# Moving buffers in SBUF: parameters in front, split weights 32 bytes apart modulo 512

## What is computed

```python
# layer 1
h = rms_norm(x, pre_mix_norm)
proj = h @ w_in                       # 1024 x 6688, split into q,k,v,z,... of two recurrences
mix = concat([gated_delta_rule(...), ssd(...)]) @ w_out
x = x + rms_norm(mix, post_mix_norm)
u = causal_dwconv(rms_norm(x, pre_ffn_norm) @ w_up, ffn_conv_w, ffn_conv_b)   # 1024 x 5632
gate, up = split(u, 2)
x = x + rms_norm((silu(gate) * up) @ w_down, post_ffn_norm)                   # 2816 x 1024
# layers 2 and 3: stick-breaking attention with pooling, then gated linear attention,
# each followed by the same kind of feed-forward block
```

## Time and profile before

| | |
|---|---|
| timed runs | 2160.79, 2166.26, 2170.13 us (median 2166.26) |
| profiled execution: span from first to last instruction | 2157.8 us |
| its own time outside the span | not recorded; the median of the timed runs is 8.5 us above the span |
| matmul engine busy | 2109.7 us, 9,776 matmuls |
| weight loads busy | 1698.0 us, beside the matmuls |
| DVE, ACT, POOL busy | 1213.1, 906.3, 325.6 us |
| DMA | 188.96 MB, 27.6% of 16 engines' time |

### The profile page before, as it was taken

How to read it: one execution, slowest core, us unless ns; L and a number is a source line. 1 busy time by engine, 2 the same in 40 slices (tenths; PEclk the granted TensorE clock), 3 DMA queues, 4 the chain that set the end, 5 groups by cost and what they waited for, 6 DMA issues and landing times.

```text
span 2157.8 us, 26841 instructions
## 1 busy us (share of the span) xinstructions
PE 2109.7 (98%) x9776; PEld 1698.0 (79%) x9776; DVE 1213.1 (56%) x1663; ACT 906.3 (42%) x1282; POOL 325.6 (15%) x266
## 2 busy tenths in 40 slices
PE   6999999999999999999999999999999999999999
PEld 5778888878868888877766888888878878888887
DVE  5898755765366665226544566653354465666522
ACT  6883445434254444224564444442242354444311
POOL 0002121220122222001302122210000011222100
PEclk9999999999999999999999999999999999999999
DMA  7323322122323233221111333232222122323321
GB/s 234 93 77 92 86 74 69 59 69 69 101 65 97 94 94 120 94 86 59 59 40 50 97 94 94 95 116 96 80 77 88 51 78 88 98 97 97 114 94 66
DMA packets 81481, 188.96 MB, mean 88 GB/s; under 512 B 19824, under 2 KB 40432, under 8 KB 81392
## 3 DMA queue, kind: packets, MB, share of 16 engines
q1 hardware_dynamic: 81392, 187.75, 27.6%
HBM read 178.28 MB, written 9.44 MB: 87 GB/s over the span
## 4 chain that ended last, share of the span: by engine, by line
PE 92%; DVE 4%; ACT 2%; issue 1%; DMA 0%; POOL 0%; SPq 0%; ACTq 0%; DVEq 0%; POOLq 0%
PE acc L253 23%; PE acc L255 23%; PE acc L254 23%; PE bank L1726 1%; PE bank L1245 1%; PE bank L229 1%; PE bank L230 1%; PE bank L231 1%; PE acc L2634 1%; PE acc L2633 1%; PE acc L2632 1%; PE bank L2017 1%; PE bank L253 1%; PE bank L255 1%; PE bank L254 1%
## 5 line engine op out<-in xcount | busy, mean ns | idle before, releaser
L253 PE MATMUL acc<-HH,whi 128*128 128x512 f32 x1600 | 642.1, 401 | 7.1 <-DVE wlo L191 4.5
L255 PE MATMUL acc<-HH,wlo 128*128 128x512 f32 x1600 | 624.4, 390 | 0.0
L254 PE MATMUL acc<-HL,whi 128*128 128x512 f32 x1600 | 623.5, 390 | 0.0
L185 ACT ACTIVATE whi<-raw 128x1024 fp32r<-128x1024 f32 (+1 forms) x293 | 324.2, 1108 | 573.5 <-PE acc L255 543.4
L191 DVE TENSOR_TENSOR wlo<-raw,whi 128x1024 fp32r<-128x1024 f32 (+1 forms) x293 | 400.9, 1369 | 287.8 <-ACT whi L185 287.8
L253 PEld LDWEIGHTS acc<-HH,whi 128*128 128x128 f32 x1600 | 301.1, 188 | 74.1 <-DVE wlo L191 11.0
L255 PEld LDWEIGHTS acc<-HH,wlo 128*128 128x128 f32 x1600 | 300.5, 188 | 64.0
L254 PEld LDWEIGHTS acc<-HL,whi 128*128 128x128 f32 x1600 | 301.1, 188 | 62.0 <-issue 4.1
L253 PE MATMUL acc<-FH,whi 128*128 128x512 f32 x528 | 208.9, 396 | 0.0
L255 PE MATMUL acc<-FH,wlo 128*128 128x512 f32 x528 | 208.6, 395 | 0.0
L254 PE MATMUL acc<-FL,whi 128*128 128x512 f32 x528 | 208.5, 395 | 0.0
(11 more groups left out here) (394 smaller groups left out, 2673.1 us busy)
## 6 DMA issues: line engine op xcount, KB each, us to landing
raw<-w SPq DMA_DIRECT2D x257, 512.0 KB, 3.5
raw<-w SPq DMA_DIRECT2D x48, 704.0 KB, 4.0
X<-x SPq DMA_DIRECT2D x4, 512.0 KB, 5.2
x_dram<-small SPq DMA_DIRECT2D x8, 256.0 KB, 4.4
xt_dram<-small SPq DMA_DIRECT2D x8, 256.0 KB, 3.6
a_dram<-l_am SPq DMA_DIRECT2D x8, 256.0 KB, 3.7
l_xt<-xt_dram SPq DMA_DIRECT2D x8, 256.0 KB, 3.5
l_x<-x_dram SPq DMA_DIRECT2D x8, 256.0 KB, 3.3
```

Of the source, the lines that this page charges most:

```text
L185: nc.scalar.activation(hi[:, 0:kt * P], raw[u % RAW][:, 0:kt * P], ACT.Copy).then_inc(w_hi_ready, 1)
L253: nc.tensor.matmul(a[:, :], wh, tile(hi, k), start=start and k == 0, stop=False)
L254: nc.tensor.matmul(a[:, :], wh, tile(lo, k), start=False, stop=False)
L255: last = nc.tensor.matmul(a[:, :], wl, tile(hi, k), start=False, stop=stop and k == kt - 1)
```

## The change

In the fixed area par, cst and small come first, ahead of X. The four split-weight buffers each get 32 bytes in front of them. FREE is the end of the fixed area, without rounding. Nothing else is changed: the instructions, their order, the queues and the waits are the same.

```diff
+        par = fixed("par", [P, cols.n])
+        cst = fixed("cst", [P, 15 * P])
+        small = fixed("small", [P, small_in.shape[1]])
         X = fixed("X", [P, KD * S])
         base_h = top[0]
         HH = fixed("HH", [P, KD * S], F32R)
         HL = fixed("HL", [P, KD * S], F32R)
         Y = nc.alloc_sbuf_tensor_at("Y", [P, KD * S], F32, offset=base_h)
         raw = [fixed(f"raw{j}", [P, HALF * P]) for j in range(RAW)]
-        whi = [fixed(f"whi{j}", [P, HALF * P], F32R) for j in range(SPLIT)]
-        wlo = [fixed(f"wlo{j}", [P, HALF * P], F32R) for j in range(SPLIT)]
-        par = fixed("par", [P, cols.n])
-        cst = fixed("cst", [P, 15 * P])
-        small = fixed("small", [P, small_in.shape[1]])
-        FREE = (top[0] + LINE - 1) // LINE * LINE
+        def apart(name):
+
+            top[0] += 32
+            return fixed(name, [P, HALF * P], F32R)
+
+        whi = [apart(f"whi{j}") for j in range(SPLIT)]
+        wlo = [apart(f"wlo{j}") for j in range(SPLIT)]
+        FREE = top[0]
```

## The result

The changed kernel takes 2175.31 us in the median of 8 runs (2171.5 to 2178.0), the kernel before 2164.1 us in 8 (2158.6 to 2170.6): ratio 1.0046, 95% interval 1.0029 to 1.0063. By the ratio it is 10 us slower; the forecast was 25 us slower. The direction was right and so was the place of the loss, the size was two and a half times too large, and the down projection moved where the forecast let it stand.

What follows compares the result with a forecast made beforehand. The matmul engine bounds the kernel: number of 512-column fp32r matmuls times the distance of their starts. +26 (matmul distances) - 1 (splits) + 0 (loads) = +25 us on the 2166.26 us median gives 2191 us; range 2126 to 2202.

Steps and rivals of the forecast that it cites:

- the change doesn't do it: Rival, matmul stream: distances go with tiles, not addresses, or gain and loss cancel; 2166 us, chance 0.14.
- Part 1, first bullet: HH and HL against split weights, 5,304 matmuls: lose the short distance, costing 32.6 us, or 17.6 in proportion.
- Part 1, second bullet: FH, DH, MH, PH against split weights, 2,160 matmuls: mixed runs gain 0, or -7.8 us in proportion.
- rows 7: Wide start of a stage: mixed rounds of nine matmuls take 233.3 ns each, so equal residues within a mixed run gain nothing.
- +26: Matmul stream: loss taken for all changed residues, chosen between +9.8 us in proportion and +32.6 if lost everywhere.
- The proportional bound: Matmul stream: price grows with byte distance; HH pairs +17.6 us, FH, DH, MH, PH pairs -7.8, sum +9.8.
- Part 2: Splits on ACT and DVE: each of 293 subtractions maybe some 100 ns shorter; on the path only -1.2 us.
- Part 3: DMA destinations: raw at worst lands 1.4 us later, hidden by buffers; input tiles 0 to +2 us; taken as 0.
- Apart is better: Rival, matmul stream: streams started 32 to 128 bytes apart collide less; middle 2140 us, chance 0.27.
- no stall left: Rival, matmul stream: separating the addresses removes the stall entirely; -110 us, 2056 us, chance 0.06.
- The low end of the range: Whole kernel: 2126 us, set by the rival that separated addresses are better, with its end; stall-free case left out.
- the second rival: Matmul stream: separated addresses remove the stall entirely; -110 us, or -94 with the skill's 216 ns; 2056 us, chance 0.06.

Runs made afterwards that it cites:

- experiment 3: Two layouts against the kernel before: parameters ahead, all residues equal, 2152.16 us, ratio 0.9935; then 128 bytes added ahead of whi0, HH pairs 128 apart, 2174.0 us, 1.0037.
- experiment 1: Kernel of matmuls alone, layer stack left out, weights at varied byte distances past the moving tile: 226.8 ns between starts at 0, 233.2 at 32.
- the first half of the change alone: Against the kernel before, only par, cst and small moved ahead of X; no gaps between split buffers, FREE still rounded: 2168.07 us, ratio 1.0007.

## Why the prediction was right in direction and wrong in size

**What bounds the kernel, and what the distance hangs on: right.** The distance of starts is what changed, and the addresses set it: the up projection lost its 226.7 ns as foretold. Swapping the residues swaps the stages (experiment 3), so the rival "the change doesn't do it" is out. One reading went too far: the matmuls counted make 7,752 x 227 to 233 ns = 1,777 us, 82% of the span and not nearly all of the engine's time.

The Trainium skill, "SBUF — State Buffer", section "Who interferes with whom", gives the matmul engine two independent read ports and says that it never waits on anyone. By that the addresses should cost nothing, and experiment 1 differs: 226.8 against 233.2 ns, with every other engine still. Whether the two reads disturb each other at the ports, or something else makes the stall, no run shows.

**Part 1, first bullet (HH pairs): mis-sized.** The price was to be that of 128 apart, 32.6 us, or in proportion, 17.6. The measured term is 20.2. A uniform 32, 64 or 96 would have cost 6.4 to 7.4 ns (experiment 1), and uniform distances are what the earlier trace rows price; but the change makes no uniform distance. It makes two blocks of three at one and the third at another, and such a mixture costs 4.4 ns in the steady stream (231.1 against 226.7) and 3.8 over all.

**Part 1, second bullet (FH, DH, MH, PH): the step that failed.** "By rows 7 a mixed run gains nothing: 0." They gained 2.9 ns, 6.3 us. The earlier trace rows are nine matmuls of a mixture of 0 and 128, less than 4 us into a stage. For what they show, a share at distance 0, they are nearly borne out: 448/448/0 takes no less than 192 alone, and six and three only 0.4 ns less than 128 alone. The gain came from what they don't show. The units with whi1 lie 192 past the moving tile for two matmuls of three, and 192 is a cheaper distance than 128 (229.1 against 232.3 in experiment 1; 229.2 against 233.3 in the down projection). The units with whi0 alternate 160 and 224 and take 231.1, 2 ns less than either alone. So in both bullets the failing assumption is one: that every distance other than 0, alone or mixed, costs what 128 costs or nearly.

The prediction doesn't divide its +26 between the bullets. If all of it is laid to the first, then of the 12 us by which it was above the measured 14, half comes from each. The proportional bound gave +17.6 and -7.8, each within 3 us of its measured term. That was luck: 32 bytes alone cost as much as 128, and the two kinds of units in the up projection, at 32/32/96 and 64/64/128, take the same.

**Part 2 (splits): no gain at all.** The two DVE rows of the kernel after, beside the earlier trace rows:

```profile
L196 DVE TENSOR_TENSOR wlo<-raw,whi 128x1024 fp32r<-128x1024 f32 x245 | 323.1, 1320 | 150.5 <-ACT whi L190 150.5
...
L196 DVE TENSOR_TENSOR first_lo<-raw,first_hi 128x1024 fp32r<-128x1024 f32 x10 | 11.8, 1223 | 13.5 <-ACT first_hi L190 13.5
```

wlo takes 1320 ns with raw, whi and wlo 32 to 128 bytes apart, as with all at one residue. The 100 ns between the two groups aren't a matter of residues: in the swapped layout of experiment 3, where wlo has the residues that first_lo has, it takes 1320 against 1222, and with all residues equal 1319 against 1222. The traces show what goes with them instead. In that of the kernel before, the 160 subtractions into wlo of 1,024 columns beside which POOL did nothing, or under 0.05 us, average 1223 ns, and the 85 others 1500; none over 1260 ns ran without a POOL instruction beside it, and 57 of those 69 ran beside `FL<-taps,FH`. No run takes POOL's work away, so the cause is argued. The error cost the forecast 1 us only, since I had put the rest under cover.

**Part 3 (loads): right.** Raw lands in 3.6 us instead of 3.5, X in 5.3 instead of 5.2, and the first half of the change alone is level with before.

```profile
raw<-w SPq DMA_DIRECT2D x257, 512.0 KB, 3.6
...
X<-x SPq DMA_DIRECT2D x4, 512.0 KB, 5.3
```

**The rivals.** "Apart is better" needed an average of the 7,464 below 227.1; it is 231.0. At 512 columns none of the 21 uniform distances tried takes less than distance 0, the nearest being 192 bytes with 229.1. It had 0.27, and "no stall left" 0.06: 13.3 ns stay even at equal residues, and no placing that was tried wins any of the 110 us down to the floor. The low end of the range, 40 us under before, rested on "apart is better". The 216 ns named beside the second rival is, in the Trainium skill, "TensorE: Matmul & The Clock Gate", section "Back-to-back issue gap", the figure for a matmul by itself; the bf16 run comes to it (215.9), no fp32r run of 512 columns does.

**What was in the rows and I passed over.** The earlier trace rows say that equal residues are fast and that 2,160 + 288 matmuls of the kernel before don't have them. The improvement that follows, FREE at the residue of the weights, was the same reading taken one step on: 2,448 x 6 to 6.6 = 15 to 16 us, and it measured 14.

## What to carry to other kernels

Where a stream of fp32r matmuls of 512 columns bounds the kernel, read the distance of starts by pairs of tiles, compute their addresses modulo 256, and give moving tiles and weights the same residue on a 32-byte grid (0, 96, 128 and 224 modulo 256 did well here); the rounding of one pool's start to 128 cost 3% of the down projection. Spreading buffers apart is no default: at 512 columns every distance but 0 was worse. For shorter streams measure again, since at 256 columns 128 apart was the better one. A price read from one distance holds neither for another nor for a mixture of two, and a rule from a few matmuls early in a stage is to be tried in a steady stream before a forecast rests on it.

## What the runs showed of the hardware that I had not expected

- The distance of fp32r matmuls of 512 columns depends on (weights - moving tile) modulo 256 bytes: 226.7 ns at 0, 229.1 at 192, 232 to 234 at the other multiples of 32, with no other engine at work.
- Even at the best it is 512/2.4 + 13.3 ns, and 120.0 for 256 columns, where 128 apart is faster (118.6); bf16 takes 215.9 for 512, with both operands at 0 modulo 256. At 1.2 GHz the same fp32r matmul takes 427.5, which is its 512 columns and next to no stall, though its tiles are 128 apart.
- The same residues can settle at 231.1 or at 232 to 233 ns; what chooses is open.
- Equal residues alone aren't enough: both at 4 bytes gives 237.7, both at 48 gives 233.2; both at 0, 224 and 352 give 226.7 to 226.8. What separates these is open; 224 and 352 are multiples of 32, 4 and 48 are not, and no more was tried. What in the engine or the memory makes the stall is open as well.
- The time spent at 1.2 GHz differs between executions of one kernel, and its time with it, by 11 us (2159.2 at a mean clock of 0.998, 2170.2 at 0.991), as much as this change.
